# Up-projection of a streaming encoder's feed-forward layer: weight sums on another engine, norm factors by another layout, other orders at the start

## The chip, the cores and the metric

One core of a Trainium2 chip runs the whole program in one launch. The metric is the device time of that launch in microseconds (us), here the median of three runs. Its engines are TensorE (PE in the rows; PEld is its weight load), VectorE (DVE), ScalarE (ACT), GpSimd (POOL) and SyncE (SP), each with an instruction queue of its own that it works off in order; they wait for one another by semaphores.

## What is computed

One layer of a hybrid encoder for 1024 prompt tokens and 64 sample tokens (1088 in all), model width 1024. The part around the change is the end of the mixer and the start of the feed-forward block, in fp32:

```python
x = x + (merged @ w_out)
y = x * lax.rsqrt(jnp.mean(x * x, axis=-1, keepdims=True) + EPS) * g      # rmsnorm(x, norm_ffn_g)
up = y @ w_up                                                            # (1088, 1024) @ (1024, 2 * 2816)
conv = conv_b + full[:, 0:L] * conv_w[0] + full[:, 1:1 + L] * conv_w[1] + full[:, 2:2 + L] * conv_w[2]
gate, val = jnp.split(conv, 2, axis=-1)
x = x + (jax.nn.silu(gate) * val) @ w_down                               # then a last rmsnorm
```

## The kernel before

The changed function, `out_engines`, writes the queues of all five engines for the last third of the program: out-projection, second norm, up-projection with convolution, down-projection, last norm. Channels lie on the 128 partitions, tokens along the free dimension. The 1088 tokens are two *halves* n = 0 and 1, each of two chunks c of 272 tokens.

**Products.** Each fp32 matrix product is made in three passes of high and low parts (`three_pass`, line 156): weight high by activation high, high by low, low by high. The up-projection pairs a gate tile with a value tile of 128 columns each (44 tiles, 22 *blocks* j) and takes the pair, with two token chunks and two halves of the contraction, as a 2x2 by 2x2 block product with seven multiplications (`product(j, i, n)`, i = 0 to 6) in place of eight. Each product is 12 matmuls of 272 columns. Its left factor is a *weight form* (`up_forms`), its right one an *activation form* (`x_forms`, for the second half `x_forms1a` for forms 0 to 3 and `x_forms1b` for 4 to 6). Forms 0, 4 (and for weights 6) are plain blocks; weight forms 1, 2, 3, 5 are sums of blocks (`up_sum`), made one out of the other; activation forms 1, 2, 3, 6 are sums called terms (`x_term`, `term(n, step)`). ScalarE rounds each form to its high part (`w_high`, `x_high`), and another engine subtracts that from the source to get the low part (`w_low`, `plain_low`, `x_low`).

**The start.** Out-projection runs in 16 steps s (8 for each half). After each, VectorE adds the residual (`residual`), ScalarE squares the sum and VectorE adds the squares into `n_acc` (`square_add`). SyncE stores each result to HBM. The first half's forms and block 0's weight forms are made between these steps. Then block 0 is done apart: seven products for half 0, then seven for half 1, while the second half's norm and forms are still being made. From block 1 on, both halves follow each other in each product.

**The second half's norm.** Two matmuls with a matrix of ones put the sum of squares, per token, on all partitions in PSUM (`norm_sum`, line 2636); ScalarE takes the root (line 2799), VectorE the reciprocal (line 3005), of 272 elements per partition and chunk; VectorE then scales the 8 channel tiles of each chunk (`x_norm1`, line 3016, 16 instructions).

**What sets the order.** Everything is written out by hand. VectorE evicts the products: `evict_v`, then c22, c11, c12, c21, and product 5 of a half may not begin before v of that half, nor product 6 before c22 (both write onto banks that these read). v reads `part_u`, a copy by ScalarE made after product 3 (`copy_u2`). In blocks 0 and 1, VectorE makes the weight sums and the plain low parts as well:

```python
        for f in X_LOW_POOL:          # GpSimd: low parts of the second half's forms 0 and 1
            x_low(f)
        for j in range(2, NF):        # GpSimd: from block 2 on
            sum3(j)
            plain_low(j, 0)
            sum1(j)
            sum2(j)
            sum4(j)
            plain_low(j, 4)
            plain_low(j, 6)
```

`x_low` on GpSimd is line 2615, the weight sums are lines 2591 to 2605, the plain low parts line 2610. On VectorE `residual` is line 2992, `square_add` 3001, `term` 3023 to 3036, `x_low` 3046, `tap` (convolution) 3126, `gated` 3135.

## Time and profile before

| | us |
|---|---|
| median of three runs | 1783.09 |
| lowest, highest | 1782.85, 1784.12 |
| span of the profiled execution, first to last instruction | 1779.1 |

Of the profiled execution only the span is given; what lies around it, against the median, is 4.0 us. The page's first part gives each engine's busy time; TensorE is the busiest. A timeline lists instructions by start, with the idle time before each in brackets and the instruction that ended it. All times named below are in us from the span's start, in that execution. A duration there is from the start to the end of an instruction, so two in a row overlap a little; matmuls of 272 columns follow each other every 0.125 us, while each is shown as 0.29 us long.

### The profile page before, as it was taken

How to read it: one execution, taken by the hardware profiler on the slowest of the kernel's cores; microseconds unless marked ns; L12 is line 12 of the kernel's file. 1: busy time of each engine (PE TensorE's matmuls, PEld its weight loads, DVE VectorE, ACT ScalarE, POOL GpSimd, SP SyncE). 2: the span in 40 equal slices, each digit the busy share in tenths (PEclk: the TensorE clock that was granted, in tenths of full speed). 3: DMA queues.
4: the chain of work that ended last, by engine and by line, in shares of the span. 5: the costliest groups of instructions: out<-in, count | busy, mean ns of one | idle time of the engine just before them, and what ended most of it. 6: DMA issues, size and time to landing. Idle time of an engine off the chain costs nothing.

```text
span 1779.1 us, 31534 instructions
## 1 busy us (share of the span) xinstructions
PE 1731.8 (97%) x12453; PEld 1665.8 (94%) x12453; DVE 1237.5 (70%) x1905; ACT 643.3 (36%) x1242; POOL 673.2 (38%) x471
## 2 busy tenths in 40 slices
PE   7999999999999999999999989999999999999997
PEld 7999999888888889989999979999999999999997
DVE  6788663676765566554574589777777777698685
ACT  5210013565652222250012434444444444534343
POOL 4554434333345667422333223555444554000000
PEclk9999999999999999999999999999999999999999
...
GB/s 276 186 124 132 237 99 245 176 168 167 165 106 134 151 108 97 101 189 235 187 141 172 98 91 51 96 73 74 74 73 73 73 74 62 357 343 279 92 192 90
DMA packets 249318, 260.72 MB, mean 147 GB/s; under 512 B 50674, under 2 KB 202974, under 8 KB 248723
## 3 DMA queue, kind: packets, MB, share of 16 engines
...
q8 instruction: 100, 1.64, 0.4%
...
## 4 chain that ended last, share of the span: by engine, by line
PE 53%; DVE 6%; DMA 3%; issue 3%; ACT 2%; POOL 1%; POOLq 0%; SPq 0%; ACTq 0%; DVEq 0%
PE bank L156 50%; DMA act_raw<-act_scratch 2%; DMA down_raw<-in_w_down 1%; PE bank L1956 1%; PE bank L1971 1%; PE bank L1976 1%; DVE x_forms L3046 0%; PE bank L1941 0%; DMA gate<-gate_scratch 0%; DVE merged L2259 0%; DVE conv L3126 0%; DVE y_t L3202 0%; DVE xt L3016 0%; POOL up_forms L2610 0%; DVE x L2196 0%
## 5 line engine op out<-in xcount | busy, mean ns | idle before, releaser
L156 PE MATMUL bank<-act_hi,w_hi 128*128 128x364 f32 (+1 forms) x1296 | 436.1, 336 | 4.5 <-POOL w_lo L878 1.7
L156 PE MATMUL bank<-act_lo,w_hi 128*128 128x364 f32 (+1 forms) x1296 | 425.6, 328 | 0.0
L156 PE MATMUL bank<-act_hi,w_lo 128*128 128x364 f32 (+1 forms) x1296 | 425.2, 328 | 0.0
L156 PEld LDWEIGHTS bank<-act_hi,w_hi 128*128 128x128 f32 x1296 | 243.6, 188 | 20.0 <-issue 10.8
L156 PE MATMUL bank<-x_forms,up_forms 128*128 128x272 f32 x1848 | 258.3, 289 | 3.6 <-DVE part_v L3094 2.0
L156 PEld LDWEIGHTS bank<-x_forms,up_forms 128*128 128x128 f32 x1848 | 242.2, 188 | 4.7 <-DVE up_forms L3078 2.3
L156 PEld LDWEIGHTS bank<-act_lo,w_hi 128*128 128x128 f32 x1296 | 243.7, 188 | 0.1
L156 PEld LDWEIGHTS bank<-act_hi,w_lo 128*128 128x128 f32 x1296 | 243.2, 188 | 0.0
L156 PE MATMUL bank<-act_form,down_form 128*128 128x272 f32 x1848 | 233.3, 288 | 2.7 <-DVE down_form L3177 1.4
L156 PEld LDWEIGHTS bank<-act_form,down_form 128*128 128x128 f32 x1848 | 231.6, 188 | 3.5 <-issue 1.6
L2610 POOL TENSOR_TENSOR up_forms<-up_w_raw,up_forms 128x512 fp32r<-128x512 f32 x60 | 88.2, 1469 | 190.7 <-ACT up_forms L2825 190.7
L156 PE MATMUL bank<-x_forms1a,up_forms 128*128 128x272 f32 x1056 | 149.5, 292 | 6.9 <-POOL x_forms1a L2615 5.7
L156 PEld LDWEIGHTS bank<-x_forms1a,up_forms 128*128 128x128 f32 x1056 | 140.5, 191 | 7.7 <-issue 7.5
L3126 DVE SCALAR_TENSOR_TENSOR conv<-up_raw,cw,conv 128x1090 f32<-128x1090 f32 x88 | 119.9, 1364 | 10.0 <-ACT conv L2855 7.3
L2825 ACT ACTIVATE up_forms<-up_sum 128x512 fp32r<-128x512 f32 x88 | 55.5, 632 | 177.4 <-POOL up_sum L2591 69.1
L3078 DVE TENSOR_TENSOR up_forms<-up_sum,up_forms 128x512 fp32r<-128x512 f32 x88 | 79.2, 902 | 51.9 <-ACT up_forms L2825 51.8
L156 PE MATMUL bank<-x_forms1b,up_forms 128*128 128x272 f32 x792 | 109.4, 287 | 0.0
L156 PEld LDWEIGHTS bank<-x_forms1b,up_forms 128*128 128x128 f32 x792 | 103.1, 188 | 0.2
L156 PE MATMUL bank<-merged_hi_lo,w_hi 128*128 128x272 f32 x512 | 97.2, 289 | 2.4 <-issue 1.1
L876 POOL CAST w_hi<-w_raw 128x1024 fp32r<-128x1024 f32 x30 | 39.9, 1330 | 143.9 <-PE bank L156 143.0
L156 PEld LDWEIGHTS bank<-merged_hi_lo,w_hi 128*128 128x128 f32 x512 | 80.3, 188 | 3.4 <-issue 1.4
L878 POOL TENSOR_TENSOR w_lo<-w_raw,w_hi 128x1024 fp32r<-128x1024 f32 x30 | 79.8, 2662 | 2.4
...
## 6 DMA issues: line engine op xcount, KB each, us to landing
...
w_raw<-in_w_in SPq DMA_DIRECT2D x44, 512.0 KB, 4.9
up_w_raw<-in_w_up SPq DMA_DIRECT2D x44, 512.0 KB, 5.0
...
w_raw<-in_w_out SPq DMA_DIRECT2D x14, 512.0 KB, 4.4
```

The source lines that it names most:

```text
L156: mm = pe.matmul(out, w(k), x(k)[:, c0:c0 + cn], start=first and k == ks[0] and n == 0, stop=last and k == ks[-1] and n == 2, skip_group_c ...
L876: pool.tensor_copy(m.wh[:, a], m.raw[:, a]).then_inc(s.w_hi, 1)
L878: pool.tensor_tensor(m.wl[:, a], m.raw[:, a], m.wh[:, a].bitcast(F32), ALU.subtract).then_inc(s.w_split, 1)
L1956: mm = pe.matmul(r4[:, g // 4, g % 4 * NCH:(g % 4 + 1) * NCH], et[:, 2 * g + h, 0:P], u2[:, j, 2 * g + h], start=h == 0, stop=h == 1)
L1971: pe.matmul(out, u2[:, j, 2 * g + 1, frames], tm1[:, g], start=True, stop=False, tile_position=(0, c))
L1976: mm = pe.matmul(out, sc[:, g, frames], cl[:, g, 1:C + 1], start=False, stop=True, tile_position=(0, c))
L2610: pool.tensor_tensor(wv[:, i, 1], a_block(j, row, col), wv[:, i, 0].bitcast(F32), ALU.subtract).then_inc(w_lo_pool, 1)
L2825: act.activation(wv[:, i, 0], src, ACT.Copy).then_inc(w_hi, 1)
L3078: dve.tensor_tensor(wv[:, i, 1], (s_even if SUM_LO[i] % 2 else s_odd)[:], wv[:, i, 0].bitcast(F32), ALU.subtract).then_inc(w_lo, 1)
L3126: dve.scalar_tensor_tensor(out=cv[:, a], in0=up[:, a, t:UP - 2 + t], scalar=m.cw01[:, 44 * t + f:44 * t + f + 1], in1=cv[:, a], op0=ALU.mu ...
```

## The change

It has four parts.

1. **Weight sums of block 1 by GpSimd** (and all three plain low parts of block 1). The four sums have a buffer each now, where two were used in turn, and GpSimd makes the four of a block one after the other, ahead of its three plain low parts, in blocks 1 to 21. For block 1 they stand ahead of its low parts of activation forms. VectorE keeps block 0's.
2. **The second half's norm factors by tokens on partitions.** Five matmuls with `n_acc` as weights and one column of ones give the sums of 128 tokens each in one column; ScalarE takes the root of 5 columns, VectorE the reciprocal; five VectorE instructions scale the identity matrix by a column each (diagonals, written over `n_acc`), and two matmuls with ones spread these over all partitions. The sums now stand behind product 0 and the spreading behind product 1.
3. **The last residual sooner.** At step 14 VectorE makes only one sum and one low part, the others at step 15 and later; one of these sits between the last residual and the addition of its squares.
4. **Other orders.** Block 0's second half does its products as 0, 4, 1, 2, 3, 5, 6; its forms, evictions and copies follow; GpSimd makes the low parts of four forms of the second half (0, 4, 1, 5) where it made two.

The diff at its core:

```diff
-X_HIGH = ((0, 4, 5, 1, 2, 3, 6), (0, 5, 1, 2, 4, 3, 6))
-X_LOW = ((0, 1, 2, 4, 3, 5, 6), (2, 4, 3, 5, 6))
-X_LOW_POOL = (0, 1)
+X_HIGH = ((0, 4, 5, 1, 2, 3, 6), (0, 4, 1, 2, 5, 3, 6))
+X_LOW = ((0, 1, 2, 4, 3, 5, 6), (2, 3, 6))
+X_LOW_POOL = (0, 4, 1, 5)
+FIRST_ORDER = (0, 4, 1, 2, 3, 5, 6)
+NORM_TILES = (0, 128, 256, 384, CH * 2 - 128)
-EVICTS_FIRST = ("v0", "c22_0", "c11_0", "c12_0", "c21_0", "v1", "c22_1", "c11_1", "c12_1", "c21_1")
+EVICTS_FIRST = ("v0", "c22_0", "c11_0", "c12_0", "c21_0", "c11_1", "v1", "c22_1", "c12_1", "c21_1")
...
+        def weight_sums(j):
+            a11, a21, a12, a22 = a_block(j, 0, 0), a_block(j, 1, 0), a_block(j, 0, 1), a_block(j, 1, 1)
+            pool.wait_ge(*raw_loaded(j))
+            pool.wait_ge(w_lo, 4 * j - 3)
+            pool.tensor_tensor(w_sum[0][:], a11, a21, ALU.subtract).then_inc(sum_made, 1)
+            pool.wait_ge(w_lo, 4 * j - 2)
+            pool.wait_ge(*sum_of(j - 1, 3))
+            pool.tensor_tensor(w_sum[1][:], a21, a22, ALU.add).then_inc(sum_made, 1)
...
+        weight_sums(1)
         for f in X_LOW_POOL:
             x_low(f)
-        for j in range(2, NF):
-            sum3(j)
-            plain_low(j, 0)
-            sum1(j)
-            sum2(j)
-            sum4(j)
-            plain_low(j, 4)
-            plain_low(j, 6)
+        for j in range(1, NF):
+            if j > 1:
+                weight_sums(j)
+            for i in PLAIN_LO:
+                plain_low(j, i)
...
+        def norm_sum1():
+            pe.wait_ge(sq_added, 14)
+            pe.wait_ge(x_sum, 2 * KD + 2)
+            for t, c0 in enumerate(NORM_TILES):
+                mm = pe.matmul(inv[1][:, 0, t:t + 1], nacc[:].rearrange("p c t -> p (c t)")[:, c0:c0 + P], m.ones[:, 0:1],
+                               start=True, stop=True)
+            mm.then_inc(sum_done, 1)
+
+        def norm_spread1():
+            for c in range(2):
+                pe.wait_ge(diag_done, 3 + 2 * c)
+                pe.matmul(inv[1][:, c], m.ones[:], nacc[:, c], start=True, stop=True).then_inc(spread, 1)
...
         for i in range(PRODUCTS):
             product(0, i, 0)
+            if i == 0:
+                norm_sum1()
             if i == 1:
-                norm_sum(1)
-        for i in range(PRODUCTS):
+                norm_spread1()
+        for i in FIRST_ORDER:
             product(0, i, 1)
...
+        def norm_inv1():
+            dve.wait_ge(root_done, 3)
+            dve.reciprocal(inv5[:], root5[:]).then_inc(inv_done, 1)
+            dve.wait_ge(inv_done, 3)
+            for t, c0 in enumerate(NORM_TILES):
+                skip = max(0, P * t - c0)
+                dve.tensor_scalar(nacc[:].rearrange("p c t -> p (c t)")[:, c0 + skip:c0 + P], m.ident[:, skip:P], inv5[:, t:t + 1],
+                                  None, ALU.mult).then_inc(diag_done, 1)
```

Three places show what moves. The first is VectorE's queue from the addition of step 14's squares (the first row) to the second half's first scaling (`xt<-xt,vec,bank`). Before (`n_acc<-n_acc,bank` adds squares, `xt<-bank,xt` is a residual, `up_forms` is a weight form's low part):

```order
L3001 TENSOR_TENSOR n_acc<-n_acc,bank 128x544
L3068 TENSOR_TENSOR up_sum_7178<-up_w_raw_7186,up_sum_7177 128x512
L3074 TENSOR_TENSOR up_forms<-up_w_raw_7186,up_forms 128x512
L3078 TENSOR_TENSOR up_forms<-up_sum_7177,up_forms 128x512
L3074 TENSOR_TENSOR up_forms<-up_w_raw_7186,up_forms 128x512
L3078 TENSOR_TENSOR up_forms<-up_sum_7178,up_forms 128x512
L3074 TENSOR_TENSOR up_forms<-up_w_raw_7186,up_forms 128x512
L2992 TENSOR_TENSOR xt<-bank,xt 128x544
L3001 TENSOR_TENSOR n_acc<-n_acc,bank 128x544
L3273 MEMSET up_raw 128x2 x2
L3005 RECIPROCAL bank<-bank 128x272
L3016 SCALAR_TENSOR_TENSOR xt<-xt,vec,bank 128x272 x4
```

And now:

```order
L3024 TENSOR_TENSOR n_acc<-n_acc,bank 128x544
L3093 TENSOR_TENSOR up_sum_7180<-up_w_raw_7188,up_sum_7179 128x512
L3099 TENSOR_TENSOR up_forms<-up_w_raw_7188,up_forms 128x512
L3015 TENSOR_TENSOR xt<-bank,xt 128x544
L3103 TENSOR_TENSOR up_forms<-up_sum_7179,up_forms 128x512
L3024 TENSOR_TENSOR n_acc<-n_acc,bank 128x544
L3099 TENSOR_TENSOR up_forms<-up_w_raw_7188,up_forms 128x512
L3103 TENSOR_TENSOR up_forms<-up_sum_7180,up_forms 128x512
L3032 RECIPROCAL n_inv<-n_root 128x5
L3036 TENSOR_SCALAR n_acc<-ident,n_inv 128x128 x4
L3036 TENSOR_SCALAR n_acc<-ident,n_inv 128x32
L3300 MEMSET up_raw 128x2 x2
```

The last residual stands after two instructions instead of six; the long reciprocal of 272 elements has given way to one of 5 and to five diagonals (four of 128 columns, one of 32), and two low parts of block 0's weights stand between the squares and these.

The second place is VectorE's queue from the first term of the second half on (`x_term<-...` are the terms, `x_forms1a` and `x_forms1b` low parts). Before:

```order
L3023 TENSOR_TENSOR x_term_7179<-xt 128x1088
L3027 TENSOR_TENSOR x_term_7180<-xt 128x1088
L3016 SCALAR_TENSOR_TENSOR xt<-xt,vec,bank 128x272 x4
L3084 TENSOR_TENSOR up_raw<-bank,part_p_7182 128x272
L3046 TENSOR_TENSOR x_forms1a<-x_term_7180,x_forms1a 128x1088
L3031 TENSOR_TENSOR x_term_7179<-xt,x_term_7180 128x1088
L3084 TENSOR_TENSOR up_raw<-bank,part_u_7183 128x272
L3046 TENSOR_TENSOR x_forms1b<-xt,x_forms1b 128x1088
L3046 TENSOR_TENSOR x_forms1a<-x_term_7179,x_forms1a 128x1088
L3036 TENSOR_TENSOR x_term_7180<-xt,x_term_7179 128x1088
```

And now:

```order
L3055 TENSOR_TENSOR x_term_7181<-xt 128x1088
L3109 TENSOR_TENSOR up_raw<-bank,part_p_7184 128x272
L3059 TENSOR_TENSOR x_term_7182<-xt 128x1088
L3109 TENSOR_TENSOR up_raw<-bank,part_u_7185 128x272
L3078 TENSOR_TENSOR x_forms1a<-x_term_7182,x_forms1a 128x1088
L3063 TENSOR_TENSOR x_term_7181<-xt,x_term_7182 128x1088
L3109 TENSOR_TENSOR up_raw<-bank,part_u_7185 128x272
L3068 TENSOR_TENSOR x_term_7182<-xt,x_term_7181 128x1088
L3078 TENSOR_TENSOR x_forms1a<-x_term_7181,x_forms1a 128x1088
L3109 TENSOR_TENSOR up_raw<-bank,part_p_7184 128x272
L3119 TENSOR_TENSOR part_v<-bank,part_u_7185 128x272
```

Terms 1 to 3 follow each other with only evictions and one low part between them; the low parts of forms 4 and 5 have gone to GpSimd.

The third place is GpSimd's queue from the end of the out-projection on (`w_lo` is its last weight's low part, `up_sum` the weight sums). Before:

```order
L2586 TENSOR_TENSOR w_lo<-w_raw,w_hi 128x1024 x12
L2615 TENSOR_TENSOR x_forms1a<-xt,x_forms1a 128x1088
L2615 TENSOR_TENSOR x_forms1a<-x_term_7179,x_forms1a 128x1088
L2591 TENSOR_TENSOR up_sum_7177<-up_w_raw 128x512
L2610 TENSOR_TENSOR up_forms<-up_w_raw,up_forms 128x512
L2595 TENSOR_TENSOR up_sum_7178<-up_w_raw 128x512
L2600 TENSOR_TENSOR up_sum_7177<-up_sum_7178,up_w_raw 128x512
L2605 TENSOR_TENSOR up_sum_7178<-up_w_raw,up_sum_7177 128x512
L2610 TENSOR_TENSOR up_forms<-up_w_raw,up_forms 128x512 x2
```

And now:

```order
L2594 TENSOR_TENSOR w_lo<-w_raw,w_hi 128x1024 x12
L2600 TENSOR_TENSOR up_sum_7177<-up_w_raw 128x512
L2603 TENSOR_TENSOR up_sum_7178<-up_w_raw 128x512
L2607 TENSOR_TENSOR up_sum_7179<-up_sum_7178,up_w_raw 128x512
L2610 TENSOR_TENSOR up_sum_7180<-up_w_raw,up_sum_7179 128x512
L2620 TENSOR_TENSOR x_forms1a<-xt,x_forms1a 128x1088
L2620 TENSOR_TENSOR x_forms1b<-xt,x_forms1b 128x1088
L2620 TENSOR_TENSOR x_forms1a<-x_term_7181,x_forms1a 128x1088
L2620 TENSOR_TENSOR x_forms1b<-xt,x_forms1b 128x1088
L2615 TENSOR_TENSOR up_forms<-up_w_raw,up_forms 128x512 x3
```

Four sums stand ahead of the second half's form 0, and forms 4 and 5 have joined forms 0 and 1.

## Rows read from the trace of the kernel before

**Rows 1.** The page's first part, engines over the whole span.

```profile
PE 1731.8 (97%) x12453; PEld 1665.8 (94%) x12453; DVE 1237.5 (70%) x1905; ACT 643.3 (36%) x1242; POOL 673.2 (38%) x471
```

**Rows 2.** Windows: length; busy PE, PEld, DVE, ACT, POOL; granted clock; DMA share, GB/s.

```profile
1040.00:1050.00 10.00, 8.46 (x62) 7.89 (x61) 6.23 (x13) 4.33 (x9) 0.00 (x0) 1.00 0.67 195
1060.00:1070.00 10.00, 5.44 (x27) 5.33 (x28) 10.00 (x13) 5.70 (x7) 2.50 (x1) 0.66 0.00 0
1200.00:1300.00 100.00, 100.00 (x798) 100.00 (x797) 78.59 (x106) 44.42 (x94) 49.23 (x33) 1.00 0.22 68
```

**Rows 3.** Timeline of TensorE; brackets hold the idle time and its releaser.

```profile
1043.42 1.78 PE L156 MATMUL bank<-x_forms,up_forms 128*128 128x272 f32 x12 [0.18 <-DVE up_forms L3074]
1046.56 1.75 PE L156 MATMUL bank<-x_forms,up_forms 128*128 128x272 f32 x12 [1.36 <-DVE xt L2992]
1048.15 1.08 PE L2636 MATMUL bank<-n_acc,ones 128*128 128x272 f32 x4
...
1064.56 6.81 PE L156 MATMUL bank<-x_forms1a,up_forms 128*128 128x272 f32 x36 [5.54 <-POOL x_forms1a L2615]
...
1081.99 1.74 PE L156 MATMUL bank<-x_forms1a,up_forms 128*128 128x272 f32 x12 [1.25 <-DVE up_raw L3084]
...
1093.99 1.75 PE L156 MATMUL bank<-x_forms,up_forms 128*128 128x272 f32 x12 [1.17 <-DVE part_v L3094]
...
1116.15 1.74 PE L156 MATMUL bank<-x_forms,up_forms 128*128 128x272 f32 x12 [0.79 <-DVE part_v L3094]
```

**Rows 4.** Timeline of VectorE around the second norm.

```profile
1042.08 0.68 DVE L3068 TENSOR_TENSOR up_sum<-up_w_raw,up_sum 128x512 f32<-128x512 f32 x1
...
1045.69 0.72 DVE L2992 TENSOR_TENSOR xt<-bank,xt 128x544 f32<-128x544 f32 x1
1047.10 0.72 DVE L3001 TENSOR_TENSOR n_acc<-n_acc,bank 128x544 f32<-128x544 f32 x1 [0.69 <-ACT bank L2794]
...
1049.76 1.87 DVE L3005 RECIPROCAL bank<-bank 128x272 f32<-128x272 f32 x1 [1.91 <-ACT bank L2799]
1051.66 1.72 DVE L3016 SCALAR_TENSOR_TENSOR xt<-xt,vec,bank 128x272 f32<-128x272 f32 x4
...
1056.01 3.35 DVE L3016 SCALAR_TENSOR_TENSOR xt<-xt,vec,bank 128x272 f32<-128x272 f32 x8
1059.40 1.29 DVE L3023 TENSOR_TENSOR x_term<-xt 128x1088 f32<-128x1088 f32 x1
```

**Rows 5.** Timeline of ScalarE, the small square root early in the program.

```profile
28.21 0.30 ACT L1315 ACTIVATE half_region<-half_region,eps 128x9 f32<-128x9 f32 x1
```

**Rows 6.** Timeline of SyncE's queue; transfers by line, with us to landing.

```profile
1039.07 1.01 SPq L2466 DMA_DIRECT2D up_w_raw<-in_w_up  x2
...
up_w_raw<-in_w_up SPq DMA_DIRECT2D x2, 512.0 KB, 4.6
```

**Rows 7.** First norm: VectorE (min/median/max ns), GpSimd beside it.

```profile
L1405 DVE TENSOR_SCALAR z<-ident,half_region x9: 243/648/2411, 29.3 to 36.6; 128x128 f32<-128x128 f32 x8, 128x64 f32<-128x64 f32 x1
...
31.13 2.44 POOL L1155 TENSOR_TENSOR w_lo<-w_raw,w_hi 128x1024 fp32r<-128x1024 f32 x1
```

**Rows 8.** VectorE and GpSimd timelines, end of block 1.

```profile
1107.42 3.38 DVE L3135 TENSOR_TENSOR ffn_act<-conv 128x1024 f32<-128x1024 f32 x2
...
1106.71 1.77 POOL L2610 TENSOR_TENSOR up_forms<-up_w_raw,up_forms 128x512 fp32r<-128x512 f32 x1 [8.95 <-ACT up_forms L2825]
1108.45 2.27 POOL L2591 TENSOR_TENSOR up_sum<-up_w_raw 128x512 f32<-128x512 f32 x1
```

**Rows 9.** GpSimd's form of an activation, and VectorE's beside it.

```profile
1061.92 2.50 POOL L2615 TENSOR_TENSOR x_forms1a<-x_term,x_forms1a 128x1088 fp32r<-128x1088 f32 x1 [4.78 <-ACT x_forms1a L2811]
...
1063.80 1.77 DVE L3046 TENSOR_TENSOR x_forms1a<-x_term,x_forms1a 128x1088 fp32r<-128x1088 f32 x1
```

**Rows 10.** ScalarE, the high part of two forms.

```profile
1060.73 2.31 ACT L2811 ACTIVATE x_forms1a<-x_term 128x1088 fp32r<-128x1088 f32 x2
```

**Rows 11.** Waits from 1110 to 1510: us in total, times, longest.

```profile
POOL up_forms L2610 <- ACT up_forms L2825: 180.1, 37, 9.0
```

More of the change, by code:

```diff
@@ L2316, in out_engines @@
     C = B + KD * T * 4
-    assert S == C + KD * T * 4 and B - A >= 3 * FORM
+    assert S == C + KD * T * 4 and B - A >= 3 * FORM + 16 * P
     X0 = S + KD * T * 4
@@ L2906, in scalar @@
             if s == 7:
-                norm_root(0)
+                norm_root0()
             if s == 8:
```

179 lines of the change are left out of this document (83 added, 96 removed).

## The prediction

> **What bounds the kernel now.** Read the page's first part first: TensorE is busy for 97% of the span [rows 1]. It can end sooner only where it waits or runs at its lower clock. Next, the windows: in the up-projection's steady part TensorE is busy for 100.00 of 100 us, 798 matmuls, with VectorE at 79 and GpSimd at 49 [rows 2]. Nothing that the change moves there can be felt unless it makes a wait. Between 1060 and 1070 it is busy for only 5.44 of 10 us, at a mean clock of 0.66 [rows 2]. Then the timeline of TensorE: behind the first product (1043.42) stand 1.36 us of waiting for the last residual, 5.54 for the low part of form 1 on GpSimd, 1.25 for an eviction in block 1, 1.17 and 0.79 for v in blocks 1 and 2 [rows 3]. That is 10.1. The 36 matmuls behind the 5.54 take 6.8 us where 36 x 0.125 + 0.2 = 4.7 would do: 2.1 for the lower of the two clock levels (1.2 for 2.4 GHz). The norm's own matmuls take 0.9 (four rows, 1.08 long with their overlap [rows 3]). So **13.1 us** are at stake, and no more; the change replaces this account with another.
>
> **The last residual.** Before, six VectorE instructions begin at 1042.08 and the residual at 1045.69, 0.6 us each [rows 4]. Four of them leave, 2.4 us, and out-projection ends in time (its last bank is ready when product 0 starts, 1043.4). The residual starts at 1043.3, its squares are added by 1045.4 (before 1047.10 + 0.72 = 1047.8 [rows 4]); the low part between them lies in the 0.7 for which VectorE waits for ScalarE [rows 4]. The wait of 1.36 is gone. In its place, the sums by token stand behind product 0, which ends at 1045.1: a wait of **0.4**.
>
> **The norm by tokens.** Five fp32 matmuls, two passes each, with one column: no row shows that form. Below, their ten weight loads at the pace of 0.125 us of other matmuls give 1.3; above, four passes in 0.9 give 2.3 for ten. The column count is 1, not 272, so I take **1.3**; 1 us more would hide under the next wait. The root of 5 columns takes some 0.3 [rows 5], the reciprocal of 5 no more, against 0.8 for two roots and 1.87 for each long reciprocal [rows 4], of which VectorE drops two. A diagonal takes 0.24 to 0.27 at its least [rows 7]. The two spreading matmuls cost **0.9**, as the sums did. Left alone, this would give the first factor at 1048.8, and scaling would start 2.8 us before the 1051.66 of now [rows 4].
>
> **But GpSimd is not idle there.** The raw weights of block 1 are asked for at 1039.5 and land 4.6 later [rows 6], at 1044.1; unlike before, GpSimd starts on its four sums at once. How do the two engines get on? Early in the program VectorE makes the same diagonals while GpSimd subtracts: 0.24 at the least, 0.65 in the middle, 2.41 at the most, which is as long as GpSimd's instruction of 2.44 beside them [rows 7]. At the end of block 1 GpSimd's subtraction of 512 columns, 1.2 by the 2.50 for 1088 in [rows 9], takes 2.27, and VectorE's two products of 1024 and 64 columns, 1.3 by the 1.29 for 1088 in [rows 4], take 3.38: 1107.42 waits for the one of 1106.71, then 1108.45 for VectorE, then VectorE's second piece for GpSimd. Each waits for the other's instruction, in turn [rows 8]. And VectorE's low part of 1088 columns takes 1.77, as it starts at 1063.80 and GpSimd's 2.50 ends at 1064.42 [rows 9].
>
> The Trainium skill's page "SBUF — State Buffer", section "Who interferes with whom", says that VectorE instructions with two SBUF inputs or in a 2-port mode (`tensor_scalar` among them) share an exclusive lock with GpSimd, held for the whole instruction. By that rule the sum is the one below; if the ports were shared without a lock, it would be that of the second rival. By that rule, the trace agrees: the instructions held up at 1106 to 1111 have two inputs in SBUF each, and take 2.27 and 3.38 [rows 8].
>
> So from 1044.1 on the two engines alternate: sum 1 to 1045.7, the low part of weight form 4 to 1046.3, sum 2 to 1047.4, low part 5 to 1048.0, sum 3 to 1049.2, diagonal 1, sum 4 to 1050.4, then the other diagonals (1.17 held by each sum). The third diagonal, which the first spreading waits for, is there at 1050.7; products 0 and 1 and the sums have ended by 1048.3. TensorE waits **2.4**. One more low part stands ahead of the scaling, which begins at 1051.5, against 1051.66. Of the 2.8 us gained, 2.6 are lost.
>
> **From the scaling to the forms.** VectorE then has 16 scalings (0.41 apart), two evictions and term 1: it starts at 1059.0, against 1059.4 now, the long second reciprocal (1.87) being traded for four more scalings ahead of it. ScalarE's high part (1.1 [rows 10]) and GpSimd's low part (2.5 [rows 9]) of form 1 follow, as before: ready at 1064.4, as before. Half 0's products now end later (by 0.4 + 1.3 + 2.4, less 1.36), and forms 0 and 4 of half 1, on GpSimd at 1054.4 and 1056.9 for 2.5 each, are ready when wanted. Products 0 and 4 fill the place where 5.54 stood, and **2.1** of waiting for form 1 stay.
>
> Then form 3. Term 3 overwrites form 1's source and waits for GpSimd. VectorE is at that moment making form 2's low part, held up as in [rows 9]; GpSimd asks for form 5 right behind form 1 (at 1064.5) and comes next, for 2.4; term 3 waits for that, in turn as in [rows 8], and ends at 1069.1, not 1066.8. High part 1.1, term 4 and low part 1.3 each, the first beside ScalarE: product 3 can start at 1072.0, and product 2 has ended at 1067.8. A wait of **4.2**. Product 5 now follows product 3 directly, so the copy by ScalarE (0.4) and v (0.4) with their handovers lie bare: **1.0**. Before, product 4 stood between. Product 6 waits **0.2** for its form.
>
> **Blocks 1 and 2.** VectorE has seven instructions (4.2 us) less, so the 1.25 goes; but block 1 also begins later (1078.1, where 1064.6 + 6.8 + 36 x 0.125 is 1075.9). v of block 1 waits in ScalarE's queue behind two weight forms of block 2, and these for GpSimd's first two sums, which wait for the activation function of block 0; VectorE has block 0's convolution, its product (3.4, as [rows 8] has it for block 1) and low parts of its own ahead of v. I find v ready at 1093.9, about as now; product 5 is due at 1078.1 + 10 x 1.51 = 1093.2: **0.7** in place of 1.17. In block 2 sums 1 and 2 come first, 1.3 us sooner than before, and 0.79 goes. From there on there is only room: GpSimd waits 180 us in all for ScalarE's forms [rows 11], and a plain low part of 1.3 us moved behind three sums (4.4) still has the rest of the 21 us of a block.
>
> **Sum.** 0.4 + 1.3 + 2.4 + 0.9 + 2.1 + 4.2 + 1.0 + 0.2 + 0.7 = 13.2, against 13.1: **+0.1**. There is the clock besides. It fell in a wait of 5.54 and not in one of 1.36 (1.00 in that window [rows 2]). Waits of 2.4 and 4.2 lie between; a fall costs up to 2.1, and I take half: **+1.0**. Together +1.1: 1783.1 + 1.1 = **1784.2**. The trace's span is 4.0 under the median, and I carry the difference to the median as it is.
>
> **Rivals.**
> *Forecast, no change (62%)*: -2 to +3.5, its own range 1781 to 1786.6.
> *Faster because VectorE slips in (15%)*: term 3 gets its turn before GpSimd's form 5. The margin is 1 us (GpSimd asks at 1064.5, VectorE at 1065.5); a later high part of form 5 decides it. Product 3 comes 3.1 sooner, the clock stays up: 0.1 - 3.1 = -3.0, with 1 us in v's chain -4: 1779. *Faster because the engines don't hold each other up (4%)*: also 2.4 and part of 0.7 go; -7: 1776. [rows 7] speaks against it.
> *Slower by the clock (13%)*: it falls in both waits, and the products behind each run at the lower level; +0.1 + 2 x 2.1 = +4.3: 1787.4. It decides at the first: if a wait of 2.4, soon after one of 0.4, is enough. Against it: part of what is lost behind the first wait is taken from the 2.1 that follows.
> *Slower in the steady part (3%)*: each plain low part comes late by 0.3 in 20 blocks, +6: 1789. [rows 11] speaks against it.
> *The change misses its mark (3%)*: the weights land a microsecond late, all sums fall behind the diagonals' place; within 1 of the forecast.
>
> **How the numbers follow.** Some 0.2% (3.6 us) is what a measurement of this kernel can tell from no change. Faster by more: most of the second and the third case, 17%. Slower by more: the clock and the steady part, 16%. Within: 67%. The range 1779.0 to 1787.4 leaves out the ends of the rivals, less than 2 in 10.
>
> **What would show it.** Right: residual near 1043.3; sum matmuls from 1045.5; diagonals of over 1 us with GpSimd's sums beside them; scaling at about 1051.5; waits of TensorE for GpSimd's form 1 (2) and VectorE's form 3 (4); a term of some 3.5 us. Wrong: diagonals of 0.3 throughout, term 3 of 1.3, product 3 without a wait, or any wait after block 2.

## The result, and the profile after

The changed kernel takes **1787.41 us** (median of 20 runs, 1783.31 to 1792.37), the kernel before 1783.27 (20 runs, 1779.47 to 1786.94), measured together. The ratio is 1.0022, with a 95% interval from 1.0015 to 1.0029: 3.9 us slower, where +1.1 was forecast. It is just past the 0.2% set as the bound, and on the upper edge of the stated range (1787.4). The profiled execution took 1787.09, its span 1785.3; so only 1.8 us lie around a span here, and most of the 4.0 in the table of before was probably that execution being a quick one.

The page's first part hardly moves against [rows 1]:

```profile
PE 1735.8 (97%) x12463; PEld 1670.4 (94%) x12463; DVE 1252.2 (70%) x1900; ACT 644.8 (36%) x1241; POOL 690.2 (39%) x480
```

TensorE's timeline, which answers to [rows 3] (start, length, instruction, in brackets the idle time ahead and what ended it):

```profile
1044.45 1.77 PE L156 MATMUL bank<-x_forms,up_forms 128*128 128x272 f32 x12 [0.18 <-DVE up_forms L3099]
1046.50 1.28 PE L2646 MATMUL bank<-ones,n_acc 128*128 128x1 f32 x10 [0.28 <-DVE n_acc L3024]
1047.64 1.76 PE L156 MATMUL bank<-x_forms,up_forms 128*128 128x272 f32 x12
1052.02 1.66 PE L2653 MATMUL bank<-n_acc,ones 128*128 128x272 f32 x4 [2.62 <-DVE n_acc L3036]
1053.09 9.23 PE L156 MATMUL bank<-x_forms,up_forms 128*128 128x272 f32 x60
...
1067.23 3.25 PE L156 MATMUL bank<-x_forms1a,up_forms 128*128 128x272 f32 x24 [1.90 <-POOL x_forms1a L2620]
1074.62 3.06 PE L156 MATMUL bank<-x_forms1a,up_forms 128*128 128x272 f32 x12 [4.14 <-issue]
1078.74 5.30 PE L156 MATMUL bank<-x_forms1b,up_forms 128*128 128x272 f32 x24 [1.05 <-DVE part_v L3119]
1083.88 1.67 PE L156 MATMUL bank<-x_forms,up_forms 128*128 128x272 f32 x12
```

The waits are 0.28, 2.62, 1.90, 4.14 and 1.05. The first product starts at 1044.45 and block 1 at 1083.88: **39.43 us for block 0's products, against 32.63 before** (1043.42 in [rows 3] to 1076.05). Two more rows of TensorE's timeline before, not shown there:

```profile
1057.28 1.74 PE L156 MATMUL bank<-x_forms1a,up_forms 128*128 128x272 f32 x12 [0.15 <-POOL x_forms1a L2615]
...
1076.05 1.66 PE L156 MATMUL bank<-x_forms,up_forms 128*128 128x272 f32 x12
```

Behind block 0 after the change nothing waits: none of the three waits of blocks 1 and 2 in [rows 3], 3.21 in all, is left. So 39.43 stands against 32.63 + 3.21 = 35.84, and **the difference, +3.59, is all but 0.3 of the 3.9 measured**. (The two profiled spans are 6.2 us apart. 1.0 of that lies ahead of product 0, which starts anywhere from 1043.05 to 1047.26 in the runs below, in no order that goes with their edits; 1.1 lies at the start of the down-projection.) The steady part is as full as in [rows 2]. Windows (length; busy PE, PEld, DVE, ACT, POOL; granted clock; DMA):

```profile
1050.00:1060.00 10.00, 7.98 (x47) 7.67 (x48) 8.77 (x23) 2.70 (x5) 4.80 (x4) 0.83 0.12 29
1060.00:1070.00 10.00, 8.10 (x65) 7.92 (x64) 9.14 (x10) 3.51 (x4) 7.47 (x3) 1.00 0.00 0
1070.00:1084.00 14.00, 8.81 (x42) 8.32 (x41) 10.32 (x14) 6.07 (x11) 4.57 (x3) 0.63 0.01 2
1120.00:1220.00 100.00, 100.00 (x798) 100.00 (x797) 80.66 (x103) 45.46 (x94) 49.27 (x32) 1.00 0.23 70
```

The last row has 100.00 of 100 us and 798 matmuls, as before. The clock is what differs. As it has two levels (full and half), a mean of c over a window of w us means 2 x (1 - c) x w at the half level: 3.4 us in the first window and 10.4 in the third, where before it was one fall of 6.8 (0.66 over 10 us in [rows 2]). Both falls lie behind or in a wait: the 4 spreading matmuls, behind 2.62, took 1.66 us (1.08 for 4 such in [rows 3]); the 12 behind 4.14 took 3.06 and the 24 behind 1.05 took 5.30.

VectorE's timeline (answers to [rows 4] and the second row of [rows 9]), then GpSimd's:

```profile
1044.32 0.72 DVE L3015 TENSOR_TENSOR xt<-bank,xt 128x544 f32<-128x544 f32 x1
...
1049.49 2.82 DVE L3036 TENSOR_SCALAR n_acc<-ident,n_inv 128x128 f32<-128x128 f32 x5
...
1052.88 4.17 DVE L3048 SCALAR_TENSOR_TENSOR xt<-xt,vec,bank 128x272 f32<-128x272 f32 x10
1058.25 0.44 DVE L3119 TENSOR_TENSOR part_v<-bank,part_u 128x272 f32<-128x272 f32 x1 [1.20 <-ACT part_u L2858]
...
1061.65 1.53 DVE L3055 TENSOR_TENSOR x_term<-xt 128x1088 f32<-128x1088 f32 x1
...
1065.91 2.33 DVE L3078 TENSOR_TENSOR x_forms1a<-x_term,x_forms1a 128x1088 fp32r<-128x1088 f32 x1 [0.83 <-ACT x_forms1a L2833]
1068.16 3.61 DVE L3063 TENSOR_TENSOR x_term<-xt,x_term 128x1088 f32<-128x1088 f32 x1
```

```profile
1047.08 1.73 POOL L2603 TENSOR_TENSOR up_sum<-up_w_raw 128x512 f32<-128x512 f32 x1
1048.97 1.50 POOL L2607 TENSOR_TENSOR up_sum<-up_sum,up_w_raw 128x512 f32<-128x512 f32 x1 [0.17 <-POOL up_sum L2603]
1050.62 1.26 POOL L2610 TENSOR_TENSOR up_sum<-up_w_raw,up_sum 128x512 f32<-128x512 f32 x1
...
1067.24 3.39 POOL L2620 TENSOR_TENSOR x_forms1b<-xt,x_forms1b 128x1088 fp32r<-128x1088 f32 x1 [0.15 <-ACT x_forms1b L2833]
```

The residual starts at 1044.32, 0.1 ahead of product 0, as forecast (1043.3 against a first product at 1043.42). Five diagonals take 2.82 beside GpSimd's third and fourth sums, and the scaling begins 8.43 us behind product 0's start, against 8.24 before: what the layout by tokens gains is gone. Term 3 (L3063) takes 3.61, in which GpSimd makes form 5 (3.39).

### The profile page after: what moved, and what is told of

It is laid out like the page before. It is cut to its first block, busy times and chain, and to the rows that moved or that the text cites. A ratio compares the mean times of both kernels' runs of the same rounds, so it can differ in the third digit from the quotient of the medians.

```text
span 1785.3 us, 31577 instructions
## 1 busy us (share of the span) xinstructions
PE 1735.8 (97%) x12463; PEld 1670.4 (94%) x12463; DVE 1252.2 (70%) x1900; ACT 644.8 (36%) x1241; POOL 690.2 (39%) x480
## 4 chain that ended last, share of the span: by engine, by line
PE 54%; DVE 5%; DMA 4%; issue 2%; ACT 2%; SPq 1%; POOL 1%; POOLq 0%; ACTq 0%; DVEq 0%
PE bank L156 51%; DMA act_raw<-act_scratch 2%; DMA down_raw<-in_w_down 2%; PE bank L1956 1%; DMA gate<-gate_scratch 1%; PE bank L1971 1%; PE bank L1976 1%; DVE merged L2259 1%; DVE x_forms L3078 0%; DVE prod L2252 0%; PE bank L1941 0%; DVE x L2196 0%; PE bank L1973 0%; DVE y L3254 0%; PE bank L2787 0%
## 5 line engine op out<-in xcount | busy, mean ns | idle before, releaser
L2615 POOL TENSOR_TENSOR up_forms<-up_w_raw,up_forms 128x512 fp32r<-128x512 f32 x63 | 92.6, 1469 | 212.7 <-ACT up_forms L2847 212.6
L3103 DVE TENSOR_TENSOR up_forms<-up_sum,up_forms 128x512 fp32r<-128x512 f32 x88 | 98.3, 1119 | 21.1 <-ACT up_forms L2847 21.1
```

The source lines that it names most:

```text
L2615: pool.tensor_tensor(wv[:, i, 1], a_block(j, row, col), wv[:, i, 0].bitcast(F32), ALU.subtract).then_inc(w_lo_pool, 1)
L3103: dve.tensor_tensor(wv[:, i, 1], w_sum[SUM_LO[i] - 1][:], wv[:, i, 0].bitcast(F32), ALU.subtract).then_inc(w_lo, 1)
```

## The experiments

The measure that tells kernels apart best is the one above: from product 0's start to block 1's, plus TensorE's waits in blocks 1 and 2. "Against before" is that sum less 35.84; the ratio is to the kernel before on the same chip, with its interval. 0.001 is 1.8 us. A, B and C are the theories that each expectation names.

| kernel | block 0 | waits in blocks 1, 2 | against before | ratio (95%) |
|---|---|---|---|---|
| before | 32.63 | 3.21 | 0 | 1 |
| the change | 39.43 | 0 | +3.6 | 1.0022 (1.0015 to 1.0029) |
| e1_gate | 37.44 | 0 | +1.6 | 1.0013 (1.0002 to 1.0023) |
| e2_vec5 | 36.21 | 0 | +0.4 | 1.0002 (0.9993 to 1.0011) |
| e3_both | 34.09 | 0 | -1.8 | 0.9986 (0.9977 to 0.9996) |
| e4_fill | 36.08 | 0.57 | +0.8 | 1.0004 (0.9993 to 1.0015) |
| e5_both_fill | 31.81 | 0.56 | -3.5 | 0.9982 (0.9974 to 0.9991) |
| e6_order | 36.83 | 0.19 | +1.2 | 1.0007 (0.9998 to 1.0017) |
| e7_resid | 31.03 | 3.23 | -1.6 | 0.9995 (0.9985 to 1.0004) |
| e8_tokens | 30.70 | 3.23 | -1.9 | 0.9994 (0.9984 to 1.0004) |
| e9_queue | 29.26 | 2.57 | -4.0 | 0.9977 (0.9966 to 0.9987) |
| e10_two_sums | 29.26 | 1.56 | -5.0 | 0.9963 (0.9949 to 0.9977) |
| e11_before_fill | 33.89 | 1.99 | 0.0 | 1.0000 (0.9989 to 1.0011) |
| e12_two_fill | 28.07 | 2.00 | -5.8 | 0.9969 (0.9957 to 0.9982) |

The two columns agree within 1.6 us. Part of their difference lies where the down-projection starts, and goes with no edit: there TensorE waits for a weight form, whose high part ScalarE makes when the raw tile's transfer lands (ScalarE waited 6.29 us for `down_raw` in the changed kernel, to 1540.87). The same wait in the changed kernel and in e7_resid:

```profile
1542.37 7.81 PE L156 MATMUL bank<-act_form,down_form 128*128 128x272 f32 x60 [2.46 <-DVE down_form L3202]
```

```profile
1535.84 14.36 PE L156 MATMUL bank<-act_form,down_form 128*128 128x272 f32 x113 [0.77 <-DVE down_form L3177]
```

It was 1.38 before and from 0.77 to 3.16 in the others, in no order that goes with their edits.

### GpSimd's sums and form 5: e1 to e3

e1_gate, on the changed kernel:

```diff
+        pool.wait_ge(spread, 1)
         weight_sums(1)
```

> The change, with one edit: GpSimd starts its four sums for block 1 only when the first spreading matmul of the norm is through (a wait ahead of the sums), so that they lie beside VectorE's scalings, which have one input in PSUM and ran at 0.41 us apart whatever GpSimd did. Theory A (the two engines hold each other up, and a lost microsecond there is passed on): the five diagonals take 1.3 us instead of 2.82, the low part and w_low ahead of them 0.7 instead of 1.3 to 1.8, TensorE's wait of 2.62 ahead of the spreading falls under 0.5, the scaling begins 2.3 us sooner, and all that hangs on it (terms, forms 1 and 3) too; the first fall of the clock is gone. 2.3 to 3 us faster than the change, about 1.0007 of the time before. Rival B (the wait has another cause: the norm by tokens is itself slow, ScalarE and VectorE in turn): the diagonals stay above 2 us, no gain, 1.002. Rival C (the 2.3 us are gained at the norm, but form 1 and form 3 come no sooner since GpSimd's forms 0 and 4 are pushed back by the sums): within 1 us of the change.

Measured: 2.0 us off block 0, and 1.0013. Timelines of TensorE, VectorE and GpSimd:

```profile
1048.18 1.08 PE L2654 MATMUL bank<-n_acc,ones 128*128 128x272 f32 x4
1048.90 7.94 PE L156 MATMUL bank<-x_forms,up_forms 128*128 128x272 f32 x60
```

```profile
1047.29 1.02 DVE L3037 TENSOR_SCALAR n_acc<-ident,n_inv 128x128 f32<-128x128 f32 x5
...
1048.91 4.17 DVE L3049 SCALAR_TENSOR_TENSOR xt<-xt,vec,bank 128x272 f32<-128x272 f32 x10
...
1058.26 3.23 DVE L3060 TENSOR_TENSOR x_term<-xt 128x1088 f32<-128x1088 f32 x1
...
1064.93 3.62 DVE L3064 TENSOR_TENSOR x_term<-xt,x_term 128x1088 f32<-128x1088 f32 x1
```

```profile
1048.88 1.29 POOL L2600 TENSOR_TENSOR up_sum<-up_w_raw 128x512 f32<-128x512 f32 x1 [12.23 <-PE bank L2654]
1050.13 1.29 POOL L2603 TENSOR_TENSOR up_sum<-up_w_raw 128x512 f32<-128x512 f32 x1
...
1056.79 3.56 POOL L2620 TENSOR_TENSOR x_forms1b<-xt,x_forms1b 128x1088 fp32r<-128x1088 f32 x1
1060.31 3.55 POOL L2620 TENSOR_TENSOR x_forms1a<-x_term,x_forms1a 128x1088 fp32r<-128x1088 f32 x1
```

Five diagonals take 1.02 and the first ten scalings 4.17, as in the changed kernel, though GpSimd's sums stand beside them (1.29 each, not 1.26 to 1.73). That answers A and refutes B: the norm by tokens is quick, the sums beside it made it slow. The Trainium skill's page "SBUF — State Buffer", section "Who interferes with whom", says that a VectorE instruction with at most one input in SBUF and outside the 2-port modes doesn't contend with GpSimd; by that rule the trace agrees, for a scaling's other input is in PSUM. The fall behind the spreading is gone, the one behind the 4.14 isn't: term 3 still takes 3.62.

C holds in part too. Term 1 starts 4.2 us sooner against product 0 (1056.38 here), but form 1 comes only 2.2 sooner. GpSimd, started late, has no pause from 1048.88 on: form 4 (3.56) stands beside term 2 (3.23 for 1.28) and holds form 1 back until 1060.31, though its high part had ended at 1059.13. So the sums slowed no scaling, but they were not free: they filled GpSimd's queue.

e2_vec5, on the changed kernel:

```diff
-X_LOW = ((0, 1, 2, 4, 3, 5, 6), (2, 3, 6))
-X_LOW_POOL = (0, 4, 1, 5)
+X_LOW = ((0, 1, 2, 4, 3, 5, 6), (2, 3, 5, 6))
+X_LOW_POOL = (0, 4, 1)
...
         evict_c11(0, 1)
+        x_low(1, 5)
```

> The change, with one edit: form 5's low part of half 1 goes back to VectorE, behind form 3's low part and an eviction; GpSimd then makes 0, 4 and 1 only. Theory A (term 3 took 3.61 us since it waited for GpSimd's form 5, and the long wait of 4.14 brings on the second fall of the clock, whose price is paid on top of the wait): term 3 takes 1.3, the wait ahead of product 3 falls from 4.14 to about 1.8, and the 36 matmuls behind it run at their full rate, 5.0 us instead of 8.36; 2.3 + 3.4 = 5.7 us faster than the change, 0.999 of the time before. Rival B (the clock has nothing to do with it, only the wait counts): 2.3 us faster than the change, 1.001. Rival C (what GpSimd doesn't hold up, the next thing does: term 3 waits for GpSimd's form 1 anyway, and VectorE has 1.3 more to do ahead of v): term 3 under 2 us, but less than 1 us gained.

Measured: 3.2 us off block 0. Timelines of VectorE, then TensorE:

```profile
1066.71 1.28 DVE L3063 TENSOR_TENSOR x_term<-xt,x_term 128x1088 f32<-128x1088 f32 x1
```

```profile
1070.84 2.06 PE L156 MATMUL bank<-x_forms1a,up_forms 128*128 128x272 f32 x12 [1.80 <-issue]
1073.96 5.47 PE L156 MATMUL bank<-x_forms1b,up_forms 128*128 128x272 f32 x24 [1.05 <-DVE part_v L3119]
```

Term 3 takes 1.28 and the wait 1.80: A's and B's 2.3 came to the tenth. Of A's 3.4 for the clock only 0.9 came, so the whole lies nearer B: product 3's 12 matmuls took 2.06 instead of 3.06, but the 24 behind them 5.47, no less than 5.30. The window over this fall:

```profile
1070.00:1080.00 10.00, 8.10 (x42) 7.84 (x43) 9.02 (x14) 4.87 (x10) 3.68 (x2) 0.66 0.01 2
```

That is 6.8 us at the half level instead of 10.4, but less of it lies in a wait. A shorter wait was not enough to keep the clock up. The first fall came here as well, behind a wait of 2.60.

e3_both has both edits:

```diff
+        pool.wait_ge(spread, 1)
         weight_sums(1)
...
-X_LOW_POOL = (0, 4, 1, 5)
+X_LOW_POOL = (0, 4, 1)
```

> The change with both edits: the sums for block 1 behind the first spreading matmul, and form 5's low part of half 1 on VectorE. Theory A (both holdings and both falls of the clock): 2.3 + 2.3 + 3.4 = 8 us faster than the change, 0.9977 of the time before. Rival B (waits alone, the clock costs nothing): 4.6 us faster than the change, 0.9997. Rival C (one hides behind the other): not more than the better of the two edits alone.

Measured: 5.3 us off block 0, as 2.0 + 3.2 by themselves; 0.9986, faster than before. The two effects add, C falls. 5.3 lies nearer B's 4.6 than A's 8, which is missed by what the clock kept: 24 matmuls in 5.20.

### The clock by itself: e4, e5, e11

e4_fill, on the changed kernel (the second fill lies on product 0's sum of the second half, which product 3 adds to, so that half of block 0 isn't the reference's):

```diff
+        def fill(out, i, n, count):
+            for t in range(count):
+                pe.matmul(out, wv[:, i, 0, t % 4], form(n, i, 0)[:, t % 4], start=True, stop=True)
...
         def norm_spread1():
+            fill(by_n(0)[:, 2], 1, 0, 18)
...
+            if (j, i, n) == (0, 3, 1):
+                pe.wait_ge(p1_out, 2)
+                fill(by_n(1)[:, 0], 3, 0, 30)
```

> The change, with matmuls whose result nobody reads in two of its waits: 18 of 272 columns ahead of the first spreading (2.1 us in the wait of 2.62) and 30 ahead of product 3 of half 1 (3.5 us in the wait of 4.14). The waits of the other engines stay as they are, so what changes is only what TensorE does meanwhile. Theory A (the clock falls because TensorE stands still there, and this costs 3.4 us behind the second wait and up to 0.5 behind the first): both falls of the granted clock are gone or short, the 36 matmuls behind the second wait take 5.0 us instead of 8.36, and the kernel is 3 to 4 us faster than the change, 1.0002 of the time before. Rival B (the clock follows something else, or its loss is hidden by waits that follow): no faster than the change, 1.002, or slower by what the added matmuls run over (0.3).

Measured: 3.35 us off block 0, 0.57 of wait in block 1, together 2.8; 1.0004. TensorE:

```profile
1069.53 4.00 PE L2652 MATMUL bank<-x_forms,up_forms 128*128 128x272 f32 x30
1073.37 1.67 PE L156 MATMUL bank<-x_forms1a,up_forms 128*128 128x272 f32 x12
1076.09 3.43 PE L156 MATMUL bank<-x_forms1b,up_forms 128*128 128x272 f32 x24 [1.05 <-DVE part_v L3127]
```

The 36 matmuls took 1.67 + 3.43 instead of 3.06 + 5.30: the half level behind the second wait cost **3.3 us**, and A stands. The first fall went too: term 1 began 15.98 us behind product 0, against 17.20. That 1.2 was not seen at the end: a short fall came behind the wait for form 1 (24 matmuls in 4.76), the fill took 4.00 instead of 3.5, and product 3 started 30.1 us behind product 0, as in the changed kernel. Form 3 had been ready since 1072.25, 1.1 sooner against product 0 than there; the fill ran 1.1 over it.

e5_both_fill puts such matmuls (12, 12, 12, 6, into half 0's free bank) into e3_both's four waits:

```diff
+FILL = {4: 12, 1: 12, 3: 12, 5: 6}
...
+        def fill(count):
+            for t in range(count):
+                pe.matmul(by_n(0)[:, 0], wv[:, 6, 0, t % 4], form(0, 6, 0)[:, t % 4], start=True, stop=True)
...
+            if (j, n) == (0, 1) and i in FILL:
+                pe.wait_ge(u2_out, 1)
+                fill(FILL[i])
```

> The change with both edits of e3_both, and matmuls that nobody reads in the four waits that e3_both still has (1.76 before product 4 of half 1, 1.76 before product 1, 1.80 before product 3, 1.06 before product 5): 12, 12, 12 and 6 of them, into a bank that is free. The waits stay what they are. In e3_both the clock is at its half level from about 1070 to 1080 and the 36 matmuls of products 3, 5 and 6 take 7.5 us instead of 5.0. Theory A (the clock falls because of several short waits close together, not of one long one): no fall, 2.5 us faster than e3_both, 0.997 of the time before. Rival B (short waits of 1 to 2 us can't be the reason; something else lets it fall): the 36 matmuls take 7.5 us again, no gain, 0.9986.

Measured: 2.3 us off block 0, no fall (36 matmuls in 1.77 + 3.44), 0.56 back in block 1. The stretch bears A out; the ratio, 0.9982 against 0.9986, is too coarse to. The executions that were not profiled agree: their mean granted clock over the whole span is 0.9972 here and 0.9943 in e3_both.

e11_before_fill does it in the 5.54 of before, with the same function:

```diff
+            if (j, i, n) == (0, 1, 1):
+                pe.wait_ge(u2_out, 1)
+                fill(42)
```

> The kernel before, with 42 matmuls that nobody reads (272 columns, into a free bank) ahead of product 1 of half 1, in the wait of 5.54. Nothing else is changed. Theory A (standing still for 5.54 us costs the half clock behind it): the 36 matmuls that took 6.81 take 4.7 to 5.0, 1.9 us faster than before, 0.9989. Rival B (the clock doesn't follow the waits): 6.8 again, 1.000.

Measured: nothing (1.0000, block 0 1.26 longer, 1.22 less behind it). TensorE:

```profile
1062.70 5.43 PE L2662 MATMUL bank<-x_forms,up_forms 128*128 128x272 f32 x42
1068.37 3.29 PE L156 MATMUL bank<-x_forms1a,up_forms 128*128 128x272 f32 x24 [0.25 <-POOL x_forms1a L2615]
1073.53 1.91 PE L156 MATMUL bank<-x_forms1a,up_forms 128*128 128x272 f32 x12 [1.86 <-issue]
1075.23 6.08 PE L156 MATMUL bank<-x_forms1b,up_forms 128*128 128x272 f32 x36
```

The 24 matmuls of products 1 and 2 run at full pace, in 3.29. But product 3 then waits 1.86 for form 3, and the clock falls behind that instead. Both theories fall: the clock does follow the waits, and it cost nothing here, since **the slow matmuls of before covered a wait for form 3**. My 2.1 was not there to be had.

### The order of products: e6

```diff
-FIRST_ORDER = (0, 4, 1, 2, 3, 5, 6)
+FIRST_ORDER = (0, 1, 2, 3, 4, 5, 6)
```

with the second half's c11 eviction behind v and c22.

> The change, with half 1's products of block 0 in the order 0 to 6 again, as before the change (and the evictions in the order that goes with it). Theory A (the order decides little: form 3 sets when product 3 starts, and product 4 then lies in the place of the 1.05 of waiting for v): the wait for form 1 grows from 1.90 to 3.4, that for form 3 stays 4.1, the one for v goes; 0.5 us slower than the change, more if the longer waits let the clock fall further. Rival B (the order is what made the change slow, since v lies bare and product 4 no longer bridges the wait): 1 us or more faster than the change, 1.0015 or less.

Measured: 2.4 us off, 1.0007: B. TensorE:

```profile
1054.01 1.19 PE L2653 MATMUL bank<-n_acc,ones 128*128 128x272 f32 x4 [2.86 <-DVE n_acc L3036]
...
1068.04 4.78 PE L156 MATMUL bank<-x_forms1a,up_forms 128*128 128x272 f32 x24 [3.76 <-POOL x_forms1a L2620]
1075.41 2.56 PE L156 MATMUL bank<-x_forms1a,up_forms 128*128 128x272 f32 x12 [2.59 <-issue]
1077.77 5.42 PE L156 MATMUL bank<-x_forms1b,up_forms 128*128 128x272 f32 x36
```

The wait for form 1 grew to 3.76 (A: 3.4) and none was left for v, but the one for form 3 was 2.59 where A had 4.1: the 24 matmuls ahead of it ran partly at the half level (4.78 us, 3.25 in the changed kernel) and covered 1.5 of it at no cost. What A left out is where the half level falls. From product 3's start to block 1, 48 matmuls took 7.6 us here and 36 with v's wait 9.3 there. That product 4 standing between kept the clock up is likely, but not shown apart from the rest. The interval of the ratio (0.9998 to 1.0017) just overlaps that of the changed kernel. This execution also had no fall behind a wait of 2.86 for the diagonals, where the changed kernel had one behind 2.62; term 1 began 16.13 us behind product 0, against 17.20, and some 1 us of the 2.4 comes from that.

### The parts alone: e7 to e10, e12

e7_resid is the kernel before with the last residual and its squares ahead of four low parts.

```diff
             residual(s)
+            if s == 15:
+                w_low(0, 3)
             square_add(s)
...
                 plain_low_first(0, 0)
-                w_low(0, 3)
+            if s == 15:
                 plain_low_first(0, 4)
```

> The kernel before, with one part of the change alone: the last residual and its squares ahead of four of VectorE's low parts for block 0. GpSimd's work, the norm and the order of products are those of before. Theory A (this part is worth what my account says by itself): TensorE's wait of 1.36 falls to about 0.3, the norm's chain is 2.3 us earlier, and the wait for form 1 falls from 5.54 to 4.3; 2.3 us faster than before, 0.9987. Rival B (the residual gains only its own wait, since VectorE's low parts now lie ahead of the first reciprocal): 1 us, 0.9994. Rival C (nothing: the wait for form 1 grows by what the first one loses): 1.000.

Measured: B by the waits. The wait of 1.36 is gone, and the one for form 1 is 5.53 still, where A had 4.3. The ratio, 0.9995 (0.9985 to 1.0004), can't tell the two apart, and the stretch gives 1.6 us, between B's 1 and A's 2.3. The squares came sooner, but the norm's sums stand behind product 1 in TensorE's queue, so the norm gained only what the wait had cost: the scaling starts 6.64 behind product 0, against 8.24, that is 1.6. B's reason is not the cause: the low parts had ended before the roots were there, and the reciprocal waited 0.91 for ScalarE.

e8_tokens adds the norm's factors by tokens (the functions of the change, here left out), with two thirds of the scalings ahead of the first eviction:

```diff
-        norm_inv(1, 0)
-        normed(1)
+        norm_inv1()
+        dve.wait_ge(x2_st[1], 32 * KD)
+        dve.wait_ge(spread, 1)
         for k in range(4):
             x_norm1(k, 0)
+        dve.wait_ge(spread, 2)
+        for k in range(6):
+            x_norm1(k, 1)
         evict_v(0, 0)
         evict_c22(0, 0)
```

> The kernel before, with two parts of the change: the last residual sooner, and half 1's norm factors with tokens on partitions (six of the second scalings ahead of the first eviction). VectorE keeps the sums for block 1 and GpSimd has nothing to do beside the diagonals; forms and product order are those of before. Theory A (the norm by tokens is good, GpSimd's sums beside it spoil it): the five diagonals take 1.3 us, the scaling starts 2.5 us sooner than before, term 1 some 4 sooner, so that the wait of 5.54 falls under 2 and the clock doesn't fall: 5.4 + up to 2.1 us faster than before, 0.996 to 0.997. Rival B (the norm by tokens gains nothing by itself, as five narrow matmuls and five diagonals cost what the long reciprocals did): as e7_resid, 0.9987. Rival C (the gain is given back at form 3 or in block 1, where the products now meet VectorE's sums for block 1): the wait for form 1 is short, but new waits of 2 us and more stand behind it, 0.9985.

Measured: 0.9994, no better than e7, which is the size that B gave, but by another cause. The diagonals took 1.02, yet the wait for form 1 was 4.15. Timelines of VectorE, then ScalarE:

```profile
1056.97 2.93 DVE L3054 TENSOR_TENSOR x_term<-xt 128x1088 f32<-128x1088 f32 x1
```

```profile
1054.55 0.40 ACT L2858 ACTIVATE part_u<-bank 128x272 f32<-128x272 f32 x1 [5.32 <-PE bank L156]
...
1055.03 1.10 ACT L2833 ACTIVATE x_forms1a<-xt 128x1088 fp32r<-128x1088 f32 x1
```

Form 0's high part stands behind the copy of u2, so GpSimd's low part of it falls beside term 1, which takes 2.93 for 1.29. e9_queue takes ScalarE's order from the change:

```diff
+        x_high(1, 0)
         copy_u2(0, 0)
         hists(0)
-        x_high(1, 0)
         x_high(1, 5)
-        copy_p1(0, 1)
         x_high(1, 1)
         x_high(1, 2)
+        copy_p1(0, 1)
```

> e8_tokens with ScalarE's queue as in the change: the high part of form 0 of half 1 ahead of the copy of u2, and those of forms 1 and 2 ahead of the copy of p1. In e8_tokens form 0's high part came at 1055.0 behind the copy, GpSimd's low part of it (1056.21, 2.5 us) then stood beside term 1, which took 2.93 instead of 1.29, and form 1's high part waited behind the copy of p1 (1060.98). Theory A (that alone held up what the norm by tokens gained): term 1 in 1.3, form 1's low part 2.5 us sooner, TensorE's wait for it 4.15 down to 1.5; a wait of up to 2 for form 3 opens behind it; 2 to 3 us faster than e8_tokens, 0.9975 of the time before. Rival B (form 3 sets the end whatever form 1 does): the wait only moves from form 1 to form 3, under 1 us, 0.999.

Measured: 0.9977; term 1 back at 1.29, the wait for form 1 1.58, for form 3 1.81: A. e10_two_sums then gives GpSimd two of block 1's sums, beside the scalings:

```diff
+        pool.wait_ge(spread, 1)
...
+        pool.tensor_tensor(s_even[:], a_block(1, 0, 0), a_block(1, 1, 0), ALU.subtract).then_inc(sum_made, 1)
+        pool.tensor_tensor(s_odd[:], a_block(1, 1, 0), a_block(1, 1, 1), ALU.add).then_inc(sum_made, 1)
         for f in X_LOW_POOL:
             x_low(f)
...
-        sum_first(1, 1)
-        sum_first(1, 2)
```

> e9_queue, and GpSimd also makes the first two of the four sums for block 1, started when the first spreading is through, so that they lie beside VectorE's scalings (which don't take turns with GpSimd). VectorE has two sums less behind half 1. Theory A: the scalings keep their 0.41, form 0's low part is not later than it is needed, and of the three waits of 1.25, 1.18 and 0.80 in blocks 1 and 2 the first shrinks by up to 1.2: 1 us faster than e9_queue. Rival B (GpSimd's 2.6 us push form 0's low part beside term 1, and term 1 is held up again): the wait for form 1 grows by 1.5, 0.5 us slower than e9_queue or worse.

Measured: 0.9963, 1.0 off the sum of the table: A. This is the fastest of all by ratio, 6.6 us below before (5.0 by the sum of the table). e12_two_fill adds 12 and 12 matmuls that nobody reads in its waits of 1.59 and 1.81:

```diff
+            if (j, i, n) in ((0, 1, 1), (0, 3, 1)):
+                pe.wait_ge(u2_out, 1)
+                fill(12)
```

> e10_two_sums, with 12 matmuls that nobody reads ahead of product 1 and 12 ahead of product 3 of half 1, in its waits of 1.59 and 1.81. There the clock is at its half level for some 3.4 us behind the second wait: products 3 to 6 (48 matmuls) took 2.56 + 5.43 with their overlap, and block 1 began 7.6 us behind product 3's start. Theory A (no engine but TensorE sets the end of that stretch): 48 matmuls in 6.1, block 1 begins 6.0 to 6.2 behind product 3, 1.5 us faster than e10_two_sums, 0.9955 of the time before. Rival B (as in e11_before_fill, where the half level lay in front of a wait for form 3 that took its place): v or form 6 is late next and stands where the slow matmuls stood; under 0.5 us, 0.9963.

Measured, TensorE:

```profile
1068.68 1.78 PE L156 MATMUL bank<-x_forms1a,up_forms 128*128 128x272 f32 x12 [0.31 <-DVE x_forms1a L3090]
1070.29 5.02 PE L156 MATMUL bank<-x_forms1b,up_forms 128*128 128x272 f32 x36
```

48 matmuls in 1.78 + 5.02, where e10 took 2.56 + 5.43: block 0 is 1.2 shorter, but the wait for v in block 1 is 0.4 longer (1.18 for 0.76), so 0.8 of A's 1.5 came by the stretch. 0.9969 against 0.9963, with intervals that overlap: no verdict between the two.

## Why the prediction came out so

**Right: the waits.** Forecast 0.4, 2.4, 2.1, 4.2, 1.0, measured 0.28, 2.62, 1.90, 4.14, 1.05. The sums by token cost 1.14 (1046.50 to 1047.64; 1.3 forecast) and term 3 3.61 (3.5). GpSimd and VectorE do take turns, and that takes back what the layout and the order gain: e1 and e2 take back 2.0 and 3.2 us by moving GpSimd's work, and e3 both. That the 1.90 for form 1 came so near 2.1 is partly luck. The forecast had form 1 ready 21.0 us behind product 0 (1064.4 less 1043.4); product 1 started 22.8 behind it. Form 1 was late, and TensorE, slowed by the first fall, came late to it as well. The rivals in which VectorE slips in, or the engines don't hold each other up, did not come.

**Right: the steady part** has only room, and the 1.25 and 0.79 of blocks 1 and 2 went.

**Too much by 1.2: small terms.** Product 6's 0.2 and block 1's 0.7 did not occur. Block 1 began so late that v was ready 1.3 us ahead of its product 5 (1097.70 for 1098.98). Without the clock my sum of 13.2 measured 9.99 of waits + 1.14 + 0.9 = 12.0.

**Wrong: the clock.** The step that failed is "a fall costs up to 2.1, and I take half: +1.0". Take from 39.43 the 12.0, and 27.4 are left for the products; the same account of before leaves 32.63 - 6.90 - 0.15 - 0.9 = 24.7, of which 2.1 was the clock, so 22.6 at full pace. The half level thus cost **4.8 us** after the change, where the sum had 1.0, and 2.7 more than before, for 13.8 us at the half level against 6.8. 12.0 + 4.8 = 16.8, against 6.90 + 0.15 + 0.9 + 2.1 + 3.21 = 13.3 before: +3.6 before rounding, as it must be, since the 4.8 is what was left over. The rows give it a second time: the 64 matmuls from the spreading on took 10.30 us (1052.02 to 1062.32) and 8.66 in e1 (1048.18 to 1056.84), which is 1.6, and e4 has 3.3 for the 36, together 4.9.

I had two things wrong. The fall's length: I took the 6.8 of before, and where a second wait (1.05 for v) and slow products follow, it was 10.4. And whether its cost is covered: before it lay in front of a wait for form 3 (e11), after the change in front of nothing (e4: 3.3 us). The first fall was not free either: it delayed VectorE's evictions and so the terms, and in e4, without it, form 3 was ready 1.1 sooner. As an estimate, 39.43 - 3.3 - 1.1 = 35.0, or 35.6 with e4's wait of 0.57 for v, against 35.84 before: at full clock the change would have been about level. The turns of GpSimd and VectorE were in the forecast's sum; all but some 0.3 of the +3.6, which was not, is the clock's.

The executions that were not profiled bear this out. The mean granted clock of the whole span is 0.9928 on average over the changed kernel's 20 executions, and 0.9949 to 0.9957 over the four groups of 10 to 35 executions of the kernel before that ran beside the experiments. By the formula above that is 7.5 to 10 us more at the half level, against 7.0 in the two profiles.

The rival "slower by the clock", +4.3, had the outcome, with half its reasoning: both waits brought a fall, but the prices were 1.5 and 3.3, not 2.1 each (the 1.5 is what 3.3 leaves of 4.8). That its 1787.4 is the measured time to the tenth is luck, and so is part of how near the forecast came: 3.8 too little for the clock and 1.2 too much for small terms took each other back in part.

**The account of before.** "13.1 us are at stake" counted the 2.1 as something that could be won. By e11 it could not, unless form 3 comes sooner as well.

**Which part does what.** The residual and the norm by tokens are worth 4 us, once ScalarE's queue is in order (e7, e8, e9). GpSimd's four sums at once cost 2.0 (1.1 of it by the fall that they brought on: e4 keeps the sums, and form 1 comes 1.1 sooner), form 5 on GpSimd 3.2, the product order up to 2.4, of which some 1 is a fall that came in one profile and not in the other. What stays open: why the clock fell behind waits of 2.62 and 2.60 (e2) and not behind one of 2.86. Each is one profiled execution, and I did not repeat them.
